# A first gating iteration of plain products, PSUM slots that alternate across the parts, and squares summed on VectorE, in a float32 network with five feed-forward blocks

## The reference

```
x = x + swiglu(rmsnorm(x) * g, w_gate, w_up, w_down)      # f0, 528 tokens
x = x + pool_mixer(rmsnorm(x) * g)
x = x + swiglu(...)                                        # f1, 528 tokens
kv = mla_shared_kv(rmsnorm(x))                             # latents, rotary key
x = x + swiglu(...)                                        # f2, 512 tokens
x = x + mla_attention(...);  x = x + swiglu(...)           # f3, 512 tokens
x = mixer(rmsnorm(rmsnorm(x)));  x = x + swiglu(...)       # f4, 512 tokens

def swiglu(h, w_gate, w_up, w_down):
    return (silu(h @ w_gate) * (h @ w_up)) @ w_down        # 1024 -> 2816 -> 1024
```

## Time and profile before

| | |
|---|---|
| median of 3 runs | 2667.11 us (2659.74 to 2675.21) |
| the profiled execution | 2662.98 us, span 2661.2 us |
| TensorE busy in it | 2479.1 us, 93% of the span, 16150 matmuls |
| VectorE / ScalarE / GpSimd busy | 1567.9 / 1491.1 / 456.2 us |
| mean granted TensorE clock | 0.968 |
| memory read | 225.60 MB, 86 GB/s |

### The profile page before, as it was taken

The page is one execution under the profiler, slowest core; times in us unless marked ns, Lnnn a source line. Parts: engine busy times, 40 slices in busy tenths (PEclk is TensorE's granted clock), DMA queues, the critical chain, the costliest instruction groups (busy, mean ns, idle before and its releaser), DMA issues. The chain is left out here.

```text
span 2661.2 us, 40041 instructions
## 1 busy us (share of the span) xinstructions
PE 2479.1 (93%) x16150; PEld 2246.5 (84%) x16150; DVE 1567.9 (59%) x2096; ACT 1491.1 (56%) x1936; POOL 456.2 (17%) x462
## 2 busy tenths in 40 slices
PE   4999998999998899999989999889989999899999
PEld 4999998899998889987668989866767788699888
DVE  6564557655557755656575745562797323656555
ACT  5554555644646645647556556553655645566454
POOL 2111111111111111111011011110565111211111
PEclk7999998999999899999999999989999999999999
DMA  4857862766866668778217678665544788486776
GB/s 143 206 136 181 208 161 62 180 164 172 193 163 152 144 177 194 184 174 210 67 25 185 170 184 213 167 147 131 126 96 110 172 195 192 107 202 153 186 187 151
DMA packets 250360, 423.77 MB, mean 159 GB/s; under 512 B 12976, under 2 KB 171312, under 8 KB 250176
## 3 DMA queue, kind: packets, MB, share of 16 engines
q0 software_dynamic: 53136, 193.49, 39.2%
q1 hardware_dynamic: 197040, 227.72, 26.5%
HBM read 225.60 MB, written 2.10 MB: 86 GB/s over the span
## 5 line engine op out<-in xcount | busy, mean ns | idle before, releaser
L760 PE MATMUL ps<-xbH,wH 128*128 128x256 f32 (+1 forms) x3080 | 885.7, 288 | 109.4 <-DVE m L1822 35.0
L760 PE MATMUL ps<-xbL,wH 128*128 128x256 f32 (+1 forms) x3080 | 881.4, 286 | 0.0
L760 PE MATMUL ps<-xbH,wL 128*128 128x256 f32 (+1 forms) x3080 | 880.8, 286 | 0.0
L760 PEld LDWEIGHTS ps<-xbH,wH 128*128 128x128 f32 x3080 | 596.6, 194 | 119.7 <-issue 77.2
L587 POOL DMA_DIRECT2D wL<-raw x369 | 318.3, 863 | 2019.4 <-ACT wL L1158 1998.0
L760 PEld LDWEIGHTS ps<-xbL,wH 128*128 128x128 f32 x3080 | 595.8, 193 | 0.2
L760 PEld LDWEIGHTS ps<-xbH,wL 128*128 128x128 f32 x3080 | 595.7, 193 | 0.0
L1158 ACT ACTIVATE wL<-raw 128x1024 fp32r<-128x1024 f32 x369 | 389.7, 1056 | 328.7 <-PE ps L679 179.6
L1154 ACT ACTIVATE wH<-wS 128x1024 fp32r<-128x1024 f32 x220 | 233.5, 1061 | 568.0 <-DVE wS L1593 544.5
L1159 ACT ACTIVATE wH<-raw 128x1024 fp32r<-128x1024 f32 x370 | 387.2, 1046 | 2.0 <-DMA raw<-in_ffn_w_gate 2.0
L679 PE MATMUL ps<-aH,wH 128*128 128x264 f32 (+1 forms) x1232 | 350.2, 331 | 8.3 <-DVE aL L1741 8.3
(11 more groups left out here) (284 smaller groups left out, 3060.2 us busy)
## 6 DMA issues: line engine op xcount, KB each, us to landing
wL<-raw POOLq DMA_DIRECT2D x369, 512.0 KB, 5.7
raw<-in_ffn_w_gate SPq DMA_DIRECT2D x88, 512.0 KB, 5.9
raw<-in_ffn_w_up SPq DMA_DIRECT2D x88, 512.0 KB, 6.7
raw<-in_ffn_w_down SPq DMA_DIRECT2D x88, 512.0 KB, 5.6
raw<-in_w_in SPq DMA_DIRECT2D x56, 512.0 KB, 3.9
raw<-in_w_ffn_in SPq DMA_DIRECT2D x44, 512.0 KB, 5.6
raw<-in_w_ffn_out SPq DMA_DIRECT2D x22, 512.0 KB, 5.1
raw<-in_w_o SPq DMA_DIRECT2D x12, 512.0 KB, 5.3
```

The lines of the kernel that those rows point to most:

```text
L760: ins = nc.tensor.matmul(ps[:, 2 * s + j, 0:TH], lhs, rhs, start=p in (1, 5, 2) and k == q == 0, stop=p in (2, 3, 4) and k == KP - 1 and q ...
```

## The change

Three edits that belong together.

1. **Iteration 0 of every FFN is eight plain products.** `PLAIN` has four units g1, g2, u1, u2 (gate and up, first and second half of the contraction), each of 48 matmuls: for both token halves, with no sums of weights or activations. Gate uses slots 3 and 1, up 2 and 0; the first unit runs k outermost and waits for each activation block apart. The steady order starts with iteration 1, and the mixed blocks and x5 are made while iteration 0 runs (`first_gating`). x5 is written over the second token half of the first plain block, so it follows g1 and u1.
2. **Slots alternate across the parts.** `turn` counts the FFN's iterations on, and x takes slot 0 or 3 by it; the down product's order is (3 - x, 1, 2, x).
3. **Squares are summed on VectorE** (`add_square`), with `BY_DVE` naming the units 0 to 2 whose low half VectorE makes. GpSimd keeps the DMA issues and the taps of a convolution. The scratch tiles move to the region of `aH`/`aL`, and the latents of f2 are normalised in its iterations 1 and 2.

The first function is TensorE's, the second VectorE's; ScalarE's `first_gating` has its halves in the same order.

```
+PLAIN = ("g1", "g2", "u1", "u2")
 def turns(part, it):
-    return FIRST if part == it == 0 else STEADY
+    return PLAIN if part == it == 0 else STEADY
-BY_DVE = {0}
+BY_DVE = {0, 1, 2}
-            lows(RING)
-            squares("f0", range(KD), T1)
...
+            def first_iteration(f):
+                slots = {"g": (3, 1), "u": (2, 0)}
+                for i, p in enumerate(PLAIN):
+                    what, e = p[0], int(p[1]) - 1
+                    b = XI[(1, 2)[e]]
+                    weights(U0[st] + i)
+                    for j, k in ([(j, k) for k in range(KP) for j in range(2)] if p == "g1" else
+                                 [(j, k) for j in range(2) for k in range(KP)]):
+                        if p == "u1" and (j, k) == (1, 0) and f < 2:
+                            ffn_stats(f, 0)
...
+                        for q, (lhs, x) in enumerate(((wh, bH), (wh, bL), (wl, bH))):
+                            for half in range(2):
+                                ins = nc.tensor.matmul(ps[:, 2 * s + half, 0:TH], lhs, x[:, b + half, k, :],
...
+                    if p == "g1" and f > 2:
+                        ffn_stats(f, 0)
...
-                        x, y, z = (0, 3)[it % 2], 1, 2
+                        x, y, z = (0, 3)[turn % 2], 1, 2
+                        turn += 1
...
-                    order = (3, 1, 2, 0) if n % 2 else (0, 1, 2, 3)
+                    order = (3 - x, 1, 2, x)
...
+            def first_gating(f, gain):
+                own()
+                mix(f, 0, gain)
+                mix(f, 1, gain)
+                sums(u + RING, f"{name}:g1.1")
+                lows(u + RING)
+                if f > 2:
+                    scales(f"f{f}", T)
+                block47(f, 0)
+                mix(f, 2, gain)
+                block47(f, 1)
+                mix(f, 3, gain)
+                sums(u + 1 + RING, f"{name}:g2.1")
+                lows(u + 1 + RING)
+                if f >= 2:
+                    gates()
+                block47(f, 2)
+                block47(f, 3)
+                if f < 2:
+                    scales(f"f{f}", T)
+                    gates()
+                sums(u + 2 + RING, f"{name}:u1.1")
+                lows(u + 2 + RING)
+                for k in range(KP):
+                    block5(f, k, gain)
...
+                sums(u + 3 + RING, f"{name}:u2.1")
+                lows(u + 3 + RING)
...
-            mixed_blocks(4, ("ffn_norm_g_2",))
-            ffn(4)
+            add_square("f4", KD - 1, SEQ)
+            for k in range(KP):
+                difference(4, k)
+            ffn(4, ("ffn_norm_g_2",))
```

More of the change, by code:

```diff
@@ L137, in ffn @@
             for it in range(pairs):
+                base, order = len(out), turns(part, it)
+                if order is PLAIN:
+                    plain(st, 4)
+                    continue
                 g1, u1, u2, g2 = (len(loads) + i for i in range(4))
                 loads.extend((st, 4 * it + i) for i in range(4))
-                base, order = len(out), turns(part, it)
                 at = {p: base + i for i, p in enumerate(order)}
@@ L640, in _ @@
                 n += POOL_PACE
-            lows(U0["wo2"] + RING)
-            for j in range(4):
-                lows(U0["wo2"] + 2 * j + 2 + RING)
-                squares("f4", (2 * j, 2 * j + 1), SEQ)
             lows(NUNITS)
@@ L753, in ffn @@
                                 for k in range(KP):
-                                    if first and j == 0:
+                                    if part == 0 and it == 1 and j == 0 and p in (4, 5, 6, 7):
                                         pe.wait_ge(dve_done, at("dve", f"x{p}:f{f}:{k}"))
@@ L1244, in gating @@
                 TH = T // 2
-                first = part == it == 0
-                u = U0[st] + 7 * it
+                reads = before and (part or it > 1)
+                u = first_unit(f, part, it)
                 def copy(i, slot_name, p, name, *reads):
@@ L1294, in ffn @@
                     for it in range(n):
-                        before = gating(f, part, it, before)
+                        if part == it == 0:
+                            before = first_gating(f, own_gain)
+                        else:
+                            before = gating(f, part, it, before)
                     hidden_high(f, before)
@@ L1762, in gating @@
                     done = f"{name}:{p}.1"
-                    if p == 1 and before:
+                    if p == 1 and before and (part or it > 1):
                         up_first(f, before)
@@ L1793, in gating @@
                         do(V.tensor_tensor(t1[:, :, 0:TH], z, kept[:, 0, :, 0:TH], ALU.add), f"rd:{name}:z", f"{name}:a")
-                        if not first:
-                            gate(0)
+                        gate(0)
+                        if f == 2 and part == 0 and it == 1:
+                            latent_scales("kv", RKV, T1)
                     elif p == 4:
@@ L1800, in gating, with ffn @@
                     lows(u + i + RING)
+                    if f == 2 and part == 0 and it == 2 and p == 3:
+                        latent_rsqrt("kv", T1)
+                        own()
+                        for k in range(KKV):
+                            do(V.scalar_tensor_tensor(clat[:, k, :], clat[:, k, :], gcol("kv_latent_norm", k),
+                                                      rl[:, :], ALU.mult, ALU.mult), f"cn:{k}")
                 return name
-            def ffn(f, p=None, gain=None):
+            def ffn(f, own_gain, p=None, gain=None):
                 T = ftok(f)
@@ L1914, in _ @@
             after("dkv", 3, "dkv:2")
-            mixed_blocks(2, ("ffn1_norm1",))
+            for k in range(KP):
+                difference(2, k)
             def latent_scales(p, n, T):
```

383 lines of the change are left out of this document (178 added, 205 removed).

## The result

The changed kernel took 2585.46 us (median of 4 runs, 2576.79 to 2589.18) where the kernel before took 2663.43 in the same comparison: a ratio of 0.9697, 95% interval 0.9652 to 0.9741. The forecast was 2571, with a range of 2546 to 2616; the time lies in the range, 14 us above the forecast. The profiled execution took 2581.97 us against 2662.98, so 81.0 us are to be accounted for where 95.7 were forecast. Against the median of the kernel before in this comparison the gain is 78.0 us.

The account below looks back on a forecast made before the run. TensorE, busy 2479.1 of 2661.2 us, was taken as the bound; starts 54.7, boundaries 39.3 and edges 2.7 - 1.0 sum to 95.7 us gained: 2567.3 from the profiled 2662.98, plus 4.1 to the median, 2571.4; range 2546 to 2616.

Parts of the forecast that it names:

- The boundaries: Fifteen waits of TensorE for slot 0 across parts: 31.8 us of stall and 7.5 of clock gained, together 39.3.
- The 0.35 us left for `kept`: At nine of fifteen boundaries p6 still waits for p1 to be copied out of slot x, 0.35 us each.
- Rival B: At the boundaries the slots give nothing, VectorE's sum and lows replacing the wait: 56.4 us gained, 2611; chance 0.08.
- The starts of f2, f3 and f4: First gating matmul to p7 of iteration 1: gains of 11.2 us net in f2, 8.6 in f3, 8.0 in f4.
- the stall before p5: In iteration 1, TensorE stands 4.1 us waiting for x5, which is last in VectorE's queue.
- the latent work: f2's 4.4 us of latent work stand on VectorE ahead of u22 in iteration 2, charged with 2.2 us.
- Rival A: In the starts VectorE's queue is the limit, so they gain nothing: 41 us gained, 2626; chance 0.15.
- Rival C: In every FFN's first two iterations, shorter but more stalls keep TensorE's clock low: slower, 2746 us; chance 0.03.
- The starts of f0 and f1: p7 of iteration 1 comes at 61.3 for 80.5 in f0, 490.3 for 498.0 in f1: gains 19.2 and 7.7.
- "-1.0" behind f0: At the edge behind f0, the pool's first block meets d7's slot, a loss of 1.0 us.
- The stall that the forecast named: Behind f3 the next product waits 8.02 us for d7's slot; a quarter can go 2.7 us earlier.
- The squares: 28 additions and four copies, 22 us, move from GpSimd to VectorE; net 0 in the sum.

Follow-up runs that it names:

- the slots alone: The kernel before with only the slots' alternation across parts and the down order (3 - x, 1, 2, x): 2625.32 us, ratio 0.9856.
- an early scale: The changed kernel with the norm's scale of f0 and f1 read and rooted ahead of the low blocks and mixes 2 and 3: 2578.59 us, ratio 0.9678.
- the changed kernel's second execution: The changed kernel run again with no edit: 2586.37 us, ratio 0.9703 to the kernel before.
- the low halves on VectorE: The changed kernel with low halves of the last six weight tiles at f0's, f2's and f3's ends on VectorE, not accumulating DMAs: 2567.07 us, ratio 0.9631.
- the copy first: The changed kernel with ScalarE's copy of p1 ahead of the weight's high half at eleven boundaries between parts: 2573.19 us, ratio 0.9659.

## Why the prediction was right, and where it was off

**The boundaries** were right in mechanism, and near in size: 39.3 us forecast, 37.8 and 33.8 measured. The measured figures hold the cadence of the later parts of 512 tokens as well, which the forecast didn't know: three of them stood at 113 ns in the kernel before, two and none in the changed one. In f0 and f1, where one cadence alone occurs, six boundaries gave 15.2 us. In f0, behind 129.09 and 225.80, where the first two boundaries now lie, the clock is 1.00 and 35 matmuls pass in 4 us, against 20 and 33 in the earlier trace rows:

```profile
129.09:133.09 4.00, 4.00 (x35) 4.00 (x34) 3.83 (x6) 0.00 (x0) 0.00 (x0) 1.00 0.01 4
225.80:229.80 4.00, 4.00 (x35) 4.00 (x34) 3.83 (x6) 0.00 (x0) 0.00 (x0) 1.00 0.00 0
```

The clock over the 4 us behind all fifteen is 1.00. The 0.35 us left for `kept` at nine boundaries were there: 0.26 to 0.61 us each, 4.2 together where 3.2 were charged. (Products 7 and 4 stand in slot x too, and only product 2 in slot 2, unlike what the section on the kernel before says; the reading is not touched by it.) Rival B is excluded by the slots alone.

**The starts of f2, f3 and f4** were right to 0.5 us each in their windows: VectorE's queue, summed row by row, gave the stall before p5 (3.9 us for 4.1), and p1 of f4 began 24.7 us after the first gating matmul where 24.2 were laid out. The stretch behind f2's window, charged with 2.2 us for the latent work, grew by 3.7. Rival A's mechanism was there, since that queue sets the time of x5, but not its size. Rival C did not occur: the mean clock of these windows was 0.81 to 0.87 and is 0.96. (Its price of 2746 is the forecast and 184 us less 9 for "what I have charged", and the layout doesn't say what the 9 are; nothing hangs on it.) The Trainium skill's account of a clock that swings although TensorE is nearly always fed ("TensorE: Matmul & The Clock Gate", on PSUM queues that cycle) has no case here: in the changed kernel nine boundaries have a stall of 0.26 to 0.61 us, and the parts behind them stand at 1.00.

**The starts of f0 and f1** failed at one step: "p1 waits for the first gate until 474.8" in f1, and "first gate read at 45.7" in f0. The gates were read about when I said in f0 (45.2), but I had TensorE wait for them at p1 only. It waits 72 matmuls earlier, since the statistics stand in slot 0 and the second column block of u1 needs that slot: 16.2 us in f0 and 8.8 in f1. The windows missed by 3.2 and 6.6 us, and an early scale gave back 3.8 and 2.9.

**The edges** failed in both directions. "-1.0" behind f0 was 6.6 to 7.5 us of loss from the slots (the two halves run apart, 71.8 for 64.2 us and 62.5 for 56.0; 65.4 in the changed kernel's second execution). I asked which slot the pool's first block meets, and not whether its weights come in time when TensorE gets there sooner. That the full DMA engines make them late is shown by the low halves on VectorE. That the stalls had given these engines a rest is my reading only: their share was 1.07 before as well.

Behind f2, 4.2 us were lost. They lie in f2's last down product and the product behind it: 48.7 us before, 49.3 with the slots alone, 53.0 in the changed kernel, 53.9 with the old slots and 52.5 with the squares on GpSimd. So by elimination it is a matter of the plain iteration's part of the change; the low halves on VectorE brought it back to 49.3. Why the plain iteration makes a tile late there is open.

Behind f3 2.7 us were forecast and 9.5 and 5.4 measured. The stall that the forecast named did what it should: 8.02 us became 5.0, and it now comes after one more quarter of the product. The rest lies elsewhere in a stretch of 567 us, in which two executions of one kernel differ by 4.1, and stays open. That it came out on the good side is luck: without this surplus of 6.8 us the other misses are 21.4.

**The squares** were forecast at no net cost, and the run with them on GpSimd is equal to 0.1%.

The sum of misses in the first execution: boundaries -1.5, f0 -3.3, f1 and the edge ahead of it -9.8, f2 -1.8, the edge behind it -4.2, f3 and f4 -0.8, the edge behind f3 +6.8, together -14.6 of the 14.7 us that are missing. In the second execution of the changed kernel 23.7 are missing.

## What to carry to other kernels

A borrowed buffer has a reader and a next user; when a planned queue is laid out by durations, follow each borrowed slot to its next user too, since that one can wait earlier than the step the value is for. When stalls are taken out of the engine that sets the time, recheck what had just been in time with them: here the next stage's weight tile, which full DMA engines brought late at a stage's end. And a change in the order of work is to be measured up to a point behind which both orders have done the same: exchanging two steps of the late queue moved the stall, and a product put into the stall moved most of it behind the window that was watched.

## What the runs showed that was not expected

Matmuls of 256 columns ran at one of two cadences, 113 or 118 ns each, at a granted clock of 1.00 in both (57.28 and 59.52 us for a part of 504). In most parts the cadence held to the end, and behind a stall of about half a microsecond it was sometimes the other. It also changed without one: in the changed kernel the first unit of f2's last part ran at 113 (2.72 us) behind a part at 118, with no idle time of TensorE between, and with the copy first f3 went over from 113 to 118 in the third unit of its second part. A few us of the scatter between executions of one kernel come from this. What sets it was not found. The matmuls of 264 columns showed one cadence only, 122 ns.
